# The value half of a spatial gating unit, projected with tokens instead of channels on the partitions

## What is computed

```python
n = _rms_norm(h, norm_mix[l])
z = n @ w_in[l]                    # columns split among the mixers and gates
...
def _spatial_gating(z, norm_g, ws, b):
    B, T = z.shape[0], z.shape[1]
    u, v = jnp.split(jax.nn.gelu(z), 2, axis=-1)      # 512 + 512 columns
    v = _rms_norm(v, norm_g).reshape(B, T // SGU_CHUNK, SGU_CHUNK, SGU_GROUPS, SGU_GROUP_DIM)
    mixed = jnp.einsum('gts,bcsgk->bctgk', jnp.tril(ws), v) + b.T[None, None, :, :, None]
    return u * mixed.reshape(B, T, D_SGU)
```

## Time and profile before

| what | value |
|---|---|
| median of 3 runs | 2720.15 us |
| lowest and highest | 2715.23 and 2720.67 us |
| span of the profiled execution | 2716.9 us |
| PE busy | 2664.1 us (98%) |
| PE weight loads busy | 2137.3 us (79%) |
| DVE, ACT, POOL busy | 1326.2, 1100.5, 1230.2 us |
| mean granted clock of PE | 0.995 of full speed |

### The profile page before, as it was taken

The page is one execution under the profiler, slowest core; times in us unless marked ns, Lnnn a source line. Parts: engine busy times, 40 slices in busy tenths (PEclk is TensorE's granted clock), DMA queues, the critical chain, the costliest instruction groups (busy, mean ns, idle before and its releaser), DMA issues.

```text
span 2716.9 us, 36975 instructions
## 1 busy us (share of the span) xinstructions
PE 2664.1 (98%) x13132; PEld 2137.3 (79%) x13132; DVE 1326.2 (49%) x1834; ACT 1100.5 (41%) x1664; POOL 1230.2 (45%) x616
## 2 busy tenths in 40 slices
PE   8999999989999999999999999999899999999999
PEld 6888888766678868888888888887667788788887
DVE  5221258786535554252541212777865364543533
ACT  5322242446644454222342223434476445542222
POOL 4444456672235424444444434567522354344443
PEclk9999999999999999999999999999999999999999
DMA  4334433222224313333333353432122342233332
GB/s 133 95 99 113 115 98 87 70 55 55 55 78 117 109 47 107 94 99 95 91 95 101 93 132 92 111 79 68 49 55 63 86 124 85 62 101 101 93 100 78
DMA packets 493612, 243.41 MB, mean 90 GB/s; under 512 B 49468, under 2 KB 491174, under 8 KB 493478
## 3 DMA queue, kind: packets, MB, share of 16 engines
q1 hardware_dynamic: 492960, 241.49, 32.0%
q10 hardware_dynamic: 518, 0.13, 0.0%
HBM read 239.46 MB, written 2.10 MB: 89 GB/s over the span
## 4 chain that ended last, share of the span: by engine, by line
PE 65%; issue 16%; POOL 8%; DVE 5%; ACT 3%; POOLq 2%; DVEq 1%; ACTq 0%; DMA 0%; SPq 0%
PE pg L636 20%; PE pg L639 19%; PE pg L642 19%; POOL wL L585 7%; PE pA L706 2%; DVE convb L1740 1%; PE pA L911 1%; PE pA L858 1%; POOLq L612 1%; POOLq L614 1%; DVE prob L1902 0%; POOL wsn L610 0%; ACT prob L1156 0%; ACT wH L1156 0%; ACT hH L1156 0%
## 5 line engine op out<-in xcount | busy, mean ns | idle before, releaser
L585 POOL TENSOR_TENSOR wL<-raw,wH 128x1024 fp32r<-128x1024 f32 (+1 forms) x472 | 1084.9, 2300 | 1453.2 <-ACT wH L1156 1449.4
L636 PE MATMUL pg<-gxH,wH 128*128 128x512 f32 (+1 forms) x2448 | 960.6, 392 | 3.6 <-DVE gxL L1601 3.1
L642 PE MATMUL pg<-gxH,wL 128*128 128x512 f32 (+1 forms) x2448 | 948.7, 388 | 0.0
L639 PE MATMUL pg<-gxL,wH 128*128 128x512 f32 (+1 forms) x2448 | 944.1, 386 | 0.0
L1156 ACT ACTIVATE wH<-raw 128x1024 fp32r<-128x1024 f32 (+1 forms) x472 | 475.8, 1009 | 834.3 <-PE pg L642 673.5
L636 PEld LDWEIGHTS pg<-gxH,wH 128*128 128x128 f32 x2448 | 461.0, 188 | 110.7 <-issue 18.4
L639 PEld LDWEIGHTS pg<-gxL,wH 128*128 128x128 f32 x2448 | 461.2, 188 | 93.6 <-issue 7.1
L642 PEld LDWEIGHTS pg<-gxH,wL 128*128 128x128 f32 x2448 | 461.0, 188 | 93.2 <-issue 3.9
L642 PE MATMUL pg<-hH,wL 128*128 128x512 f32 x992 | 392.7, 396 | 0.0
L636 PE MATMUL pg<-hH,wH 128*128 128x512 f32 x992 | 390.5, 394 | 1.5 <-DVE hL L1657 1.5
L639 PE MATMUL pg<-hL,wH 128*128 128x512 f32 x992 | 390.6, 394 | 0.0
(11 more groups left out here) (234 smaller groups left out, 2208.8 us busy)
## 6 DMA issues: line engine op xcount, KB each, us to landing
raw<-in_ffn_wi SPq DMA_DIRECT2D x352, 256.0 KB, 3.1
raw<-in_w_in SPq DMA_DIRECT2D x200, 256.0 KB, 3.3
raw<-in_ffn_wo SPq DMA_DIRECT2D x128, 256.0 KB, 3.0
raw<-in_ffn_wo SPq DMA_DIRECT2D x64, 192.0 KB, 2.6
raw<-in_xkv SPq DMA_DIRECT2D x32, 256.0 KB, 3.0
raw<-in_w_out SPq DMA_DIRECT2D x32, 256.0 KB, 3.0
raw<-in_sgu_out SPq DMA_DIRECT2D x32, 128.0 KB, 2.2
raw<-in_conv_out SPq DMA_DIRECT2D x32, 128.0 KB, 2.2
```

The costliest lines, as they stand in the source:

```text
L585: pool.tensor_tensor(wL[:, s % 4, 0:n, :], raw[:, s % 2, 0:n, :], wH[:, s % 4, 0:n, :].bitcast(F32), ALU.subtract)\
L636: mm(o, wH[:, s, k, :], rh(k), start=(k == 0), stop=False)
L639: mm(o, wH[:, s, k, :], rl(k), start=False, stop=False)
L642: last = mm(o, wL[:, s, k, :], rh(k), start=False, stop=(k == kt - 1))
```

## The change

The four value units become one block, `by_token`. The inputs are stationary (128 channels by 128 tokens) and 512 weight columns move, so that each of the four banks holds 128 tokens by the 512 value channels. Row block pairs of the weights come one after the other, as rows of 512 columns, and all four banks are open until the last. ACT applies gelu straight out of PSUM with the token factor as its scale, which has been turned to the partitions by four tiny matmuls behind the convolution's units. The squares are summed by ACT as it goes, and the norm is one number a token. The products with the matrix of ones, the transposes of `v` and ACT's copies of them are gone. PE's `mixed(c)` moves from p 5, 9, 12, 15 to p 1, 5, 9, 11. DVE's order of the opening is untouched, its taps before the opening are grouped anew, and its `v` norm moves one unit ahead.

```diff
-                    unit(l, U_SGU + j, 0, cols_of(win, C_SGU + DS + j * P))
+                def row_tiles(w, c0, i):
+                    def src(h, half):
+                        return k_rows(w)[:, 2 * i + h, c0:c0 + T]
+                    return src
+                def wide(u, src):
+                    s = u % 2
+                    sp.wait_ge(split_l, risen(split_l, l, u - 1))
+                    for h in range(2):
+                        sp.dma_start(raw[:, s, 4 * h:4 * h + 4, :].rearrange("p a c -> p (a c)"),
+                                     src(h, 0)).then_inc(landed[s], 16)
+                for i in range(4):
+                    wide(U_SGU + i, row_tiles(win, C_SGU + DS, i))
...
+            def by_token(l, u0, done, behind=()):
+                for i in range(4):
+                    u = u0 + i
+                    pe.wait_ge(split_l, risen(split_l, l, u + 1))
+                    for a in range(TT):
+                        if i == 0:
+                            pe.wait_ge(evac, risen(evac, l, u0 + a - 3))
+                        o = pg[:, (u0 + a) % 4, :]
+                        at = slice(a * P, (a + 1) * P)
+                        for h in range(2):
+                            k = 2 * i + h
+                            high = wH[:, u % 4, 4 * h:4 * h + 4, :].rearrange("p a c -> p (a c)")
+                            low = wL[:, u % 4, 4 * h:4 * h + 4, :].rearrange("p a c -> p (a c)")
+                            mm(o, gxH[:, k, at], high, start=(k == 0), stop=False)
+                            mm(o, gxL[:, k, at], high, start=False, stop=False)
+                            last = mm(o, gxH[:, k, at], low, start=False, stop=(k == KD - 1))
+                        if a == TT - 1:
+                            last.then_inc(unit_mm, 1)
+                        elif i == 3:
+                            last.then_inc(done, 1)
+                    for piece in behind[i:i + 1]:
+                        piece()
...
+                pe.wait_ge(rs_ok, risen(rs_ok, l, 1))
+                for a in range(TT):
+                    last = mm(pO[:, a:a + 1], rstd[0:1, a * P:(a + 1) * P], ones[0:1, 0:1],
+                              start=True, stop=True)
+                last.then_inc(rs_mm, 1)
...
-                def v_squares(k):
-                    pe.wait_ge(vsq, risen(vsq, l, k + 1))
-                    if k == 0:
-                        pe.wait_ge(stat_rt, risen(stat_rt, l, 6))
-                    last = mm(pO, ones[:, :], sq[:, k % 2, :], start=(k == 0), stop=(k == 3))
-                    last.then_inc(vsq_mm if k < 3 else stat_mm, 1)
-                for j in range(1, 8):
+                def compressed():
...
+                    last.then_inc(cmp2, 1)
+                def key_norm():
+                    stat(l, 4, bdon, NCMP)
+                    v_rows(1)
+                by_token(l, U_SGU, v_mm,
+                         (compressed, key_norm, lambda: stat(l, 5, bdon)))
+                for j in range(4, 8):
                     unit(l, U_SGU + j, 0, KD, gH, gL)
-                    if j == 1:
-                        stat(l, 4, bdon, NCMP)
-                        v_rows(1)
-                    if j == 2:
-                        stat(l, 5, bdon)
-                    if 3 <= j < 7:
-                        v_squares(j - 3)
                 unit(l, U_Q1, 0, KD, gH, gL)
...
-                def v_turned(c):
+                def mixed(c):
                     if c == 0:
                         pe.wait_ge(vn, risen(vn, l, 1))
-                        pe.wait_ge(t_free, risen(t_free, l, 3))
-                    elif c == 3:
-                        pe.wait_ge(t_free, risen(t_free, l, 4))
-                    else:
-                        pe.wait_ge(sg_cp, risen(sg_cp, l, c))
-                    for g in range(GROUPS):
-                        last = turn(pT[:, g * P:(g + 1) * P], vG[:, g, c * P:(c + 1) * P])
-                    last.then_inc(sg_tr, 1)
-                def mixed(c):
-                    pe.wait_ge(sg_cp, risen(sg_cp, l, c + 1))
-                    if c == 0:
-                        pe.wait_ge(stat_rt, risen(stat_rt, l, 8))
+                        pe.wait_ge(stat_rt, risen(stat_rt, l, 7))
                     if c:
                         pe.wait_ge(sg_out, risen(sg_out, l, c))
                     for g in range(GROUPS):
-                        last = mm(pO[:, g * P:(g + 1) * P], sq[:, c % 2, g * P:(g + 1) * P],
+                        last = mm(pO[:, g * P:(g + 1) * P], vG[:, c, g * P:(g + 1) * P],
                                   wsT[:, g, :], start=True, stop=True)
                     last.then_inc(sg_mm, 1)
...
                 def opening(p):
-                    if p in (0, 3, 6, 10):
-                        v_turned((0, 3, 6, 10).index(p))
-                    if p in (5, 9, 12, 15):
-                        mixed((5, 9, 12, 15).index(p))
+                    if p in (1, 5, 9, 11):
+                        mixed((1, 5, 9, 11).index(p))
...
-                for j in range(8):
+                for j in range(4):
                     ahead(l, U_SGU + j)
                     if j == 1:
                         root(l, 4, rv, 1.0 / DH, NCMP)
                     if j == 3:
                         root(l, 5, rv, 1.0 / DH)
-                    if j == 7:
-                        root(l, 6, rv, 1.0 / DS)
+                act.wait_ge(rs_in, risen(rs_in, l, 1))
+                for a in range(TT):
+                    if a < TT - 1:
+                        act.wait_ge(v_mm, risen(v_mm, l, a + 1))
+                    else:
+                        act.wait_ge(unit_mm, risen(unit_mm, l, U_SGU + 4))
+                    act.activation(vG[:, a, :], pg[:, (U_SGU + a) % 4, :], ACT.Gelu_apprx_tanh,
+                                   scale=rsN[:, a:a + 1]).then_inc(evac, 1)
+                ahead(l, U_SGU + 4)
+                for j in range(4, 8):
+                    if j > 4:
+                        ahead(l, U_SGU + j)
+                    if j == 4:
+                        act.drain()
+                        for a in range(TT):
+                            act.activation(sq[:, a % 2, :], vG[:, a, :], ACT.Square,
+                                           accum_out=vss[:, a:a + 1])
+                            if a % 2:
+                                act.drain()
+                        act.activation(vss[:, :], vss[:, :], ACT.Sqrt, bias=eps[:, 0:1],
+                                       scale=1.0 / DS).then_inc(v_sum, 1)
                     act.wait_ge(evac, risen(evac, l, U_SGU + j + 1))
-                    dst = vG[:, j, :] if j < 4 else uG[:, j - 4, :]
-                    act.activation(dst, tb[:, j % 2, :], ACT.Gelu_apprx_tanh).then_inc(gelu, 1)
-                    if 1 <= j < 5:
-                        k = j - 1
-                        act.drain()
-                        if k >= 2:
-                            act.wait_ge(vsq_mm, risen(vsq_mm, l, k - 1))
-                        act.activation(sq[:, k % 2, :], vG[:, k, :], ACT.Square).then_inc(vsq, 1)
...
                 ahead(l, U_NG + 1)
...
-                    if c >= 2:
-                        act.wait_ge(sg_mm, risen(sg_mm, l, c - 1))
-                    copy(sq[:, c % 2, :], pT).then_inc(sg_cp, 1)
                 def merge_gate(n):
                     t = tb[:, n % 2, :]
...
                 root_of(l, 1, rstd)
...
                 scaled(kvc[:, 0, :], l, U_KV)
+                dve.wait_ge(rs_mm, risen(rs_mm, l, 1))
+                dve.tensor_copy(rsN[:, :], pO[:, 0:TT]).then_inc(rs_in, 1)
...
                 scaled(qT[:, 0, :], l, U_Q0)
-                conv(3)
-                scaled(tb[:, 0, :], l, U_SGU)
...
-                conv(3)
-                for j in range(2, 8):
-                    dve.wait_ge(gelu, risen(gelu, l, j - 1))
+                conv(7)
+                normed(l, 5, qT[:, 0, :], g8[:, 0:1])
+                conv(6)
+                for j in range(4, 8):
+                    if j == 4:
+                        dve.wait_ge(evac, risen(evac, l, U_SGU + TT))
+                    if j >= 6:
+                        dve.wait_ge(gelu, risen(gelu, l, j - 5))
                     scaled(tb[:, j % 2, :], l, U_SGU + j)
-                    if j == 3:
-                        normed(l, 5, qT[:, 0, :], g8[:, 0:1])
-                        conv(3)
-                    elif j == 6:
-                        root_of(l, 6, rv)
-                        for k in range(4):
-                            STT(vG[:, k, :], vG[:, k, :], col(P_SG + k), rv[:, :], ALU.mult,
+                    if j == 5:
+                        dve.wait_ge(v_sum, risen(v_sum, l, 1))
+                        dve.reciprocal(vss[:, :], vss[:, :])
+                        dve.drain()
+                        for a in range(TT):
+                            STT(vG[:, a, :], vG[:, a, :], vss[:, a:a + 1], gbc[:, :], ALU.mult,
                                 ALU.mult)
```

(15 more changed lines are left out.)

53 lines of the change are left out of this document (25 added, 28 removed).

## The result

The changed kernel takes 2733.03 us (median of 5 runs, 2726.47 to 2734.38) against 2720.15 us (5 runs, 2715.23 to 2721.66). The ratio is 1.0044, with an interval of 1.0033 to 1.0055: slower, by 0.44%. The forecast was 2719.3 us and the range ended at 2727.

What follows compares the result with a forecast made beforehand. PE, busy for 98% of the span, was taken as the bound. Terms -10.8 + 1.8 + 11.2 + 0 - 5.4 + 2.4 = -0.8 us gave a forecast of 2719.3 us, range 2710 to 2727 us.

Steps and rivals of the forecast that it cites:

- What leaves PE: On PE, products of squares with ones (-7.1 us) and transposes of v (-3.7 us) go: -10.8 us.
- the block at zero: On PE, by_token has the same 96 matmuls a layer and as many weight loads, so it adds zero.
- Rival 4: Value block: exchanged operands leave each weight load bare, 192 loads cost up to 31 us; 2750 us, chance 0.02.
- The `rsN` products: Four one-row, one-column products added on PE, 0.9 us a group: +1.8 us for two layers, bounds +1.3 and +2.0.
- The first `mixed` at zero: Opening, p 1: ACT's root of the second queries comes soon enough, so no wait is added.
- rival 3: Opening, first mixed: ACT's root comes as late as before, 2.3 us a layer; 2723.9 us, chance 0.07.
- Second and third wait: Opening, p 5 and p 9: PE waits for DVE's preceding mixed, taken as 0.8 and 2.3 us.
- The fourth wait: Opening, p 11: DVE must first take out the unit and do its mixed(2); 2.3 to 2.6 us, taken as 2.5.
- The clock: Behind the opening's new waits, one fall of the granted clock of 1.2 us a layer: +2.4 us, bounds 0 and 4.8.
- Rival 2: Opening: clock falls behind both long waits, POOL brings nothing back; +8.2 us, 2728.4 us, chance 0.11.
- What comes back: At PE's wait of 593.92, POOL's lead lets DVE's taps run faster: 2.7 us a layer, -5.4 us for two.
- The five taps that DVE does earlier: They fall out behind the wait at 593.92 and meet no wait of PE: zero.

Runs made afterwards that it cites:

- e4_before_early: The kernel before with its four mixed products at p 2, 5, 9 and 11, without the value block: 2742.26 us, 1.0077 of the kernel before.
- e1_late: The changed kernel with the four mixed products back at p 5, 9, 12 and 15: 2709.84 us, 0.9958 of the kernel before.
- e2_psum: The changed kernel with DVE's sum of mixed kept in PSUM, so no instruction reads two SBUF operands: 2721.94 us, 1.0012 of the kernel before.
- e3_fill: The changed kernel with 8 and 16 unused matmuls ahead of the third and fourth mixed: 2719.04 us, 0.9995 of the kernel before.
- e10: The kernel before with DVE's taps spread over places where DVE waited, without the value block: 2715.40 us, 0.9986 of the kernel before.
- e11: e1_late with DVE's taps spread over places where DVE waited, sums of mixed in SBUF: 2699.47 us, 0.9924 of the kernel before.

## Why the prediction was wrong

It had the mechanism of the loss and mis-sized two of its terms, both in the opening. In the whole kernel the move of `mixed` cost 22 to 23 us (e4_before_early against the kernel before, the changed kernel against e1_late), where the terms for it, waits, clock and what comes back, gave 8.2; the block brought 9 to 10 us, where its terms gave 9.0. Step by step:

- **What leaves PE, and the block at zero: right.** The value block, 96 matmuls from 475.53 to 499.41, runs in steps of 0.227 us, with longer ones only beside the small products ahead of it and between its quarters; from 494.41, in its last quarter, to 532.05 there are 166 steps, none above 0.24. The stretch to A is 2.6 us shorter in the first layer once the start of the load of x, 0.4 us later, is taken off: the forecast was -3.6 + 0.9. In the second layer it is 3.8, but that stretch varies: 1241.4 to 1244.1 us in the ten traces with the block, 1244.7 to 1245.8 in the three without. A to B of e1_late, 1.9 us under the kernel before, confirms the transposes (-1.84); in the second layer it is 3.1, since there the kernel before also waits 0.98 us for ACT. Rival 4 falls.
- **The `rsN` products: too low.** From 426.08 to 427.71, over two matmuls, they add 1.63 - 0.45 = 1.18 us, against 0.9. The bound from above, the neighbour with the same width of one column, had been 1.0. That bound was the duration of a group, and the group here lasts 1.05 us, much like its neighbour; what it adds to the path from unit to unit is more than its duration.
- **The first `mixed` at zero, rival 3: right.** It starts at 534.97 without a wait.
- **Second and third wait: right.** 0.65 and 2.06 us against 0.8 and 2.3.
- **The fourth wait: the first step that failed.** The forecast was "its `mixed(2)`, 0.77 and 0.7 to 1.0 us", and 2.5 us in all; measured 2.72 for the product and 4.18 for the wait. I had bounded the product by the rows of `mixed` in the first layer, and had followed DVE alone behind the end of the unit, not ACT and POOL, which the same matmul releases. The kernel before had such a product in its second layer, beside a low part of POOL from 1905.26 on, and the eight products together would have shown it:

```profile
1905.92 2.30 DVE L1852 TENSOR_TENSOR big<-big,tmp 128x512 f32<-128x512 f32 x1
```

  e2_psum takes the collision away, and the wait is 2.15 us.
- **The clock: the second step that failed, and the larger one.** I took one fall of 1.2 us a layer, from the stretch of 3 us behind 593.92; measured 4.4 us in the first opening, in two stretches. e3_fill shows them to be the clock's. Behind the fourth `mixed` the low clock held for some 5 us, though PE had no gap any more, and not for a part of 3. The kernel before had a longer stretch as well, which the price left out: behind its wait of 2.87 us at 604.94 the clock is 0.72 over 604 to 610, 1.7 us. Rival 2 had both falls, and they came, its sign; yet it priced each at 1.2 us as well, so even its 2728.4 us was low, though it gave nothing for what comes back.
- **What comes back: right in size, by luck; wrong in its cause.** B to C gave 3.24 and 2.38 us against 2.7. The 3.24 are 1.97 at the wait of 593.92 (2.48, now 0.51) and 1.27 at the one before it (2.38, now 1.11), which the forecast left out. POOL's low part after gate 1 no longer lags, as foretold; it waits for ACT:

```profile
569.72 1.29 POOL L603 TENSOR_TENSOR wL<-raw,wH 128x512 fp32r<-128x512 f32 x1 [6.71 <-ACT wH L1179]
```

  I called it POOL's lead from the block, with "PE's waits let it gain 4 more" as an aside. The aside was nearly all of it: without the waits POOL still lags by 4.2 us, against 7.5 before, and the block brings 0.89 us (e1_late); with the waits and no block POOL idles 7.04 us there and the return is the same (e4_before_early). It refunds a third of what the waits cost and must not be counted as the block's.
- **Not foreseen: C.** Between 593.92 and 604.94 lay 11.02 us before, and between 597.96 and 608.98 lie 11.02 us now. The chain of DVE and ACT there doesn't move, so when PE came to it sooner its wait grew from 2.87 to 4.40 us, and the low clock behind it grew from 1.7 to 2.9 us (C to D is 1.1 and 1.3 us longer).
- **"The five taps that DVE does earlier fall out behind this place and meet no wait of PE; zero": right for this kernel, wrong as a judgement of the change.** There are four of them by the traces. e10 and e11 show that they are worth some 4.5 us a layer (C to D) as soon as the chain at C is relieved.

In numbers of the first layer: opening forecast +5.0 (-1.8 + 5.6 + 1.2), measured +9.5; of the miss of 4.5 us, 1.3 are the waits and 3.2 the clock. Over the whole span the forecast was -0.8 and the two traces give +10.0: of the 10.8 between them 8.1 lie in the two openings, 2.4 in C to D, 1.1 in the last stretch, and the rest comes to -0.9. The chance of 0.11 for rival 2 was too low: the low clock behind a long wait had rows for it, and the argument against it ("POOL's lead ... hardly depends on these waits") was wrong, as e4_before_early shows.

## What to carry to other kernels

When a product is asked for earlier, the engine that feeds it must be earlier too; if its order is untouched, the move only turns slack into waits. With TensorE 98% busy such a wait can be paid twice, once idle and once in low clock: here waits of 6.9 us brought 4.4 more, though not each wait did. Price a step behind the end of a unit by all the engines that its last matmul releases, not only by the one that is waited for. A gain that a change makes on the bound engine may be hidden by the next chain: here the ratio of the block to the kernel before was 1.0044 with the new places and 0.9958 with the old ones, and the block was worth 16 us once DVE's taps lay in DVE's gaps.

## What was not expected of the hardware

- The low clock cost 4.4 us behind waits of 6.9, two thirds of them again. Filling 5.4 of these 6.9 us with useless matmuls made the kernel 8.2 us shorter by the spans, 14.0 by the medians.
- Waits of 2.05 and 2.06 us at the same place were followed by a granted clock of 1.00 in one kernel and 0.59 in the other; waits of 1.95 and 1.96 at the same place of the two layers by 0.50 and 1.00 in one execution.
- DVE's product with both operands in SBUF took 693 to 2722 ns beside POOL, and 686 to 689 ns with one of them in PSUM.
- Four products of a single row and column cost PE 1.18 us.
